# Moving the second half of each tile's projection later in a mixer's attention, and leaving out twelve products of constants

## The chip, the cores and the metric

The kernel runs on one core of one Trainium2 chip. The metric is the device time of one execution in microseconds (us).

## The reference

The model has two layers (DEPTH = 2) on 512 rows of width 1024. Each layer is a half-step feed-forward net, a mixer, and a second half-step feed-forward net, all with RMS norms around them:

```python
h = h + 0.5 * rms_norm(swiglu(rms_norm(h, g[0]), ffn1_gate[l], ffn1_up[l], ffn1_down[l]), g[1])
m = hybrid_mixer(rms_norm(h, g[2]), w_in[l], ...)
h = h + rms_norm(m, g[3])
h = h + 0.5 * rms_norm(swiglu(rms_norm(h, g[4]), ffn2_gate[l], ffn2_up[l], ffn2_down[l]), g[5])

def hybrid_mixer(u, w_in, ...):
    proj = u @ w_in                                   # 1024 -> 1796 columns
    qa, ka, va, us, qc, kc, vc, fc = jnp.split(proj, IN_SPLITS, axis=-1)
    ya = swa_sink_attention(qa, ka, va, ...)          # 8 heads, sliding window of 2 chunks of 64
    yb = s5_mixer(us, ...)                            # state-space layer, GELU and a gate (GLU)
    yc = fox_attention(qc, kc, vc, fc, ...)           # 4 heads, causal, with forget gates
    y = jnp.concatenate([rms_norm(ya, ga), rms_norm(yb, gb), rms_norm(yc, gc)], axis=-1)
    return y @ w_out
```

## The kernel before, in words

Everything is written by hand for each engine, in program order, with counting semaphores between the engines. Activations lie transposed in SBUF. Each weight is split into a high part (`wh`, ScalarE, L1046) and a low part (`wl`, VectorE, L1494), and each product of weights and activations is done as three (`three`: L559, L560, L561) into one PSUM bank, so a tile of 128 output columns is 8 steps of k with three products of 512 columns each. Most of the time goes to such products in the feed-forward nets.

The mixer's input projection has 15 column tiles (`COLS`). Tiles 0 to 8 are projected ahead of the attention. Tiles 9 to 14 (`vc0`, `kc0`, `qc0`, `kc1`, `vc1`, `qc1`: what the forgetting attention needs) are projected inside the attention loop, each as two halves of k, 12 products each (`project_half`). All six use the same PSUM bank, `ps1`, one after the other: the first half of a tile waits in `bank_free` for the semaphore that VectorE raises (L1692) when its reader of the tile before is done. The reader is `value_columns` (L1720, for `vc0` and `vc1`) or `fox_tile` (L1732, two operations, for the others).

The loop over `s` runs through 32 items of attention, 16 of the sliding window (`swa`: four head pairs by four blocks of 128 queries) and 16 of the forgetting attention (`fox`), and some steps beyond. TensorE does at step s: the scores of item s (L847 and L851, or L855 and L857, or L863 and L865), halves of tiles by table, `attend` (L905, at odd s for two items that started four and five steps earlier), and the transpose of the probabilities of item s − 3 (`turn`, L882). VectorE does the maximum of item s (L1782 to L1791 and L1795) and the normalisation of item s − 2 (L1805 to L1814), then readers, splits and parts of the state-space layer. ScalarE does the copy of the transposed probabilities of item s − 3 (L1277), the exponentials of item s (L1257 and L1262, or L1266), then copies, splits and more. The scores of item s wait for the exponentials of item s − 2, since two banks alternate. Between the items stand the state-space layer's products: `ssm_direct` at step 2 (L812, L815), `ssm_out` at step 4 (L825), whose copy by ScalarE (L1350) the scores of item 6 wait for, the gate (`glu`, L942) at step 17, and a norm's sum (`branch_sum`, L930) at step 22. At step 3 twelve products of constants into a bank that nobody reads (`spin`, L605) stand before the transpose.

Tables set what stands at which step: `PROJECT_AT` the first halves (items 0, 4, 8, 12, 16, 19). The second half of a tile stands one step after the first, its reader and the ScalarE split of a later tile's weights two steps after the first, on VectorE and ScalarE:

```python
if s in PROJECT_AT:
    project_half(PROJECT_AT[s], 0)
if s - 1 in PROJECT_AT:
    project_half(PROJECT_AT[s - 1], 1)
...
if half == 0:
    bank_free(m)
    pe.wait_ge(w_split, base + u + RAW_SLOTS + 1)
```

Of the kernel before, what the change touches and what calls it, by code (L numbers as in the profile page):

```python
# [75 lines left out]
N_COLS = len(COLS)  # L76
# [11 lines left out]
def units_of(m):  # L88

    return (m, 1) if m < TILE["fc"] else (m, 2) if m == TILE["fc"] else (m + 1, 1)  # L90
# [94 lines left out]
def build(nc, x, norm_gains, ffn1_gate, ffn1_up, ffn1_down, w_in, swa_sinks, lam_re, lam_im, log_dt,  # L185
# [8 lines left out]
    with ExitStack() as ctx:  # L194
# [332 lines left out]
        def _(pe):  # L527
# [227 lines left out]
            def mixer(l):  # L755
# [15 lines left out]
                def project_half(m, half):  # L771

                    b, place = bank_of(m)
                    u = units_of(m)[0]
# [3 lines that stand above are left out]
                    for k in range(half * (KD // 2), (half + 1) * (KD // 2)):  # L778
                        mm = three(ps[b][:, :], in_slot(u), k, k, k == 0, k == KD - 1)
                    if half:  # L780
                        mm.then_inc(unit_done, 1)
# [193 lines left out]
                for s in range(N_ITEMS + LAG_PV):  # L975
                    if s == SSM_OUT_AT - 2:
                        ssm_direct()
                    if s == SSM_OUT_AT:
                        ssm_out()
                    if s < N_ITEMS:  # L980
                        scores(s)
                    if s in PROJECT_AT:
                        project_half(PROJECT_AT[s], 0)
                    if s - 1 in PROJECT_AT:
                        project_half(PROJECT_AT[s - 1], 1)
                    if s in SPIN_AT:
                        spin(BU_BANK[0], SPIN_AT[s])
                    if s > LAG_PV and (s - LAG_PV) % 2:
                        attend(s - LAG_PV - 1)
                    if LAG_T <= s < N_ITEMS + LAG_T:  # L990
                        turn(s - LAG_T)
                    if s in VALUES_AT:
                        values(VALUES_AT.index(s))
                    if s in SUM_AT:
                        branch_sum(SUM_AT[s])
                    if s in OUT_AT:
                        out_part(0, OUT_AT[s])
                    if s == 29:
                        fox_sum(6)
                    if s == GLU_AT:  # L1000
                        glu()
# [19 lines left out]
        def _(act):  # L1021
# [185 lines left out]
            def mixer(l):  # L1207
# [29 lines left out]
                for u in range(5, N_AHEAD + 3):  # L1237
                    if u > 6:
                        split_unit(base + u, in_slot(u))
                    m = u - 3  # L1240
# [92 lines left out]
                for s in range(N_ITEMS + LAG_PV):  # L1333
# [6 lines left out]
                            pair_out(pr)  # L1340
                    if s in VALUES_AT:
                        values(VALUES_AT.index(s))
                    if s - 2 in PROJECT_AT and PROJECT_AT[s - 2] + 2 < N_COLS:
                        u = units_of(PROJECT_AT[s - 2] + 2)[0]
                        split_unit(base + u, in_slot(u))
                    if s == SSM_OUT_AT:
                        act.wait_ge(o_mm, l + 1)
# [69 lines left out]
        def _(dve):  # L1417
# [260 lines left out]
            def mixer(l):  # L1678
# [165 lines left out]
                for u in range(5, N_AHEAD + 3):  # L1844
# [3 lines left out]
                    m = u - 3  # L1848
# [22 lines left out]
                for s_ in range(N_ITEMS + LAG_N):  # L1871
                    if s_ < N_ITEMS:
                        maxes(s_)
                    if s_ >= LAG_N:
                        norms(s_ - LAG_N)
                    if s_ - 2 in PROJECT_AT:
                        m = PROJECT_AT[s_ - 2]
                        if COLS[m][0][0] == "v":
                            value_columns(m, 1 + int(COLS[m][0][2]))
                        else:  # L1880
                            fox_tile(m, [n_ for n_, _ in COLS if n_[:2] in ("kc", "qc")].index(COLS[m][0]))
# [314 lines left out]
SPLIT_BEHIND = {0: (4, 5), 4: (6,), 5: (7,)}  # L2196
OUT_SPLIT_AT = {21: 0, 22: 1, 30: 2, 31: 3}
OUT_AT = {27: (0,), 28: (1,), 29: (2,), 30: (3,), 31: (4,), 32: (5,)}
SPIN_HOLE, SPIN_AT = 18, {3: 12}
PAD = 24  # L2200
ROWS_FROM = 6

# [3 lines left out]
GELU_AT = (7, 11)  # L2206
GLU_AT = 17
GATE_STEPS = {1: ((0, 0),), 2: ((0, 1), (1, 0)), 3: ((0, 2), (1, 1)), 4: ((1, 2),)}
LOW_AT = {3: 11, 8: 12, 12: 13, 15: 14}
PROJECT_AT = {0: 9, 4: 10, 8: 11, 12: 12, 16: 13, 19: 14}  # L2210
VALUES_AT = (None, 8, 20)

# [26 lines left out]
```

## Time and profile before

| | |
|---|---|
| time, median of 3 runs (lowest, highest) | 1948.27 us (1942.56, 1949.94) |
| the profiled execution: its time, its span | 1947.21 us, 1945.3 us |
| TensorE busy | 98% of the span |
| VectorE, ScalarE, GpSimd busy | 52%, 37%, 11% |
| mean granted clock of TensorE | 0.990 of full speed |
| TensorE's share of the chain that ended last | 95% |

The span is the time from the first to the last instruction; the device time is some 2 us longer. The chain that ended last is followed back from the last instruction through whatever released each step. A granted clock of 1.0 is TensorE's upper level (2.4 GHz), 0.5 its lower (1.2 GHz).

### The profile page before, as it was taken

The page shows a single profiled execution, that of the slowest core. Times are in us where ns is not written, and L with a number is a line of the kernel's source. Part 1 is how long each engine was busy: PE and PEld are TensorE (multiplying, and loading weights), DVE is VectorE, ACT ScalarE, POOL GpSimd, SP SyncE. Part 2 cuts the span into 40 slices and gives each one's busy share as a digit, 9 for nine tenths or more (in the row PEclk, how much of TensorE's full clock was granted, in tenths as well). Part 3 has the DMA queues.
Part 4 walks back from the last instruction along what each step waited for, and adds up shares of the span by engine and source line. Part 5 has one row for each costly group of instructions (what it writes and reads, how often), then busy time and mean ns, then how long its engine had stood idle before and what let it go on. Part 6 is the DMA issues. An engine that isn't in the chain of part 4 may idle for free.

```text
span 1945.3 us, 24754 instructions
## 1 busy us (share of the span) xinstructions
PE 1909.2 (98%) x9136; PEld 1543.7 (79%) x9136; DVE 1006.3 (52%) x1429; ACT 723.1 (37%) x1134; POOL 209.9 (11%) x433
## 2 busy tenths in 40 slices
PE   8999999999999999999999999999998999999998
PEld 6888888877667888888878888887875778888887
DVE  5664432387657544432376544335876574444323
ACT  4333332255654433332243333223565453333321
POOL 2831000023100000000056100000131000000000
PEclk9999999999999999999999999999998999999999
DMA  6334343351213333343333433333502123333331
GB/s 176 108 106 127 97 119 98 85 158 55 55 46 85 104 95 96 96 118 102 99 89 98 131 98 109 105 94 98 161 25 66 55 86 99 97 97 104 109 90 44
DMA packets 330954, 188.55 MB, mean 97 GB/s; under 512 B 6996, under 2 KB 325432, under 8 KB 329848
## 3 DMA queue, kind: packets, MB, share of 16 engines
q1 hardware_dynamic: 324008, 168.13, 30.1%
q0 software_dynamic: 5824, 18.79, 3.5%
q8 instruction: 52, 0.85, 0.2%
q10 hardware_dynamic: 1040, 0.52, 0.1%
q14 instruction: 30, 0.25, 0.0%
HBM read 175.72 MB, written 11.67 MB: 96 GB/s over the span
## 4 chain that ended last, share of the span: by engine, by line
PE 95%; ACT 2%; DVE 2%; issue 1%; DMA 0%; DVEq 0%; ACTq 0%
PE ps L559 19%; PE ps L561 18%; PE ps L560 18%; PE ps L696 8%; PE ps L695 8%; PE ps L694 8%; PE ps L587 2%; PE ps L588 2%; PE ps L592 2%; PE ps L905 1%; PE ps L882 1%; PE ps L863 1%; DMA raw<-in_ffn_gate 0%; PE ps L639 0%; PE ps L855 0%
## 5 line engine op out<-in xcount | busy, mean ns | idle before, releaser
L1494 DVE TENSOR_TENSOR wl<-raw,wh 128x1024 fp32r<-128x1024 f32 (+1 forms) x265 | 350.6, 1324 | 755.9 <-ACT wh L1046 754.7
L559 PE MATMUL ps<-xh,wh 128*128 128x512 f32 x1552 | 612.4, 395 | 2.4 <-DVEq L1692 1.3
L561 PE MATMUL ps<-xh,wl 128*128 128x512 f32 x1552 | 605.3, 390 | 0.0
L560 PE MATMUL ps<-xl,wh 128*128 128x512 f32 x1552 | 605.2, 390 | 0.0
L1046 ACT ACTIVATE wh<-raw 128x1024 fp32r<-128x1024 f32 (+1 forms) x265 | 301.1, 1137 | 658.7 <-PE ps L696 341.6
L559 PEld LDWEIGHTS ps<-xh,wh 128*128 128x128 f32 x1552 | 292.0, 188 | 67.9 <-issue 3.5
L561 PEld LDWEIGHTS ps<-xh,wl 128*128 128x128 f32 x1552 | 291.8, 188 | 61.6
L560 PEld LDWEIGHTS ps<-xl,wh 128*128 128x128 f32 x1552 | 292.1, 188 | 60.1 <-issue 1.2
L694 PE MATMUL ps<-Hh,wh 128*128 128x512 f32 x704 | 274.0, 389 | 0.0
L696 PE MATMUL ps<-Hh,wl 128*128 128x512 f32 x704 | 273.9, 389 | 0.0
L695 PE MATMUL ps<-Hl,wh 128*128 128x512 f32 x704 | 273.9, 389 | 0.0
L695 PEld LDWEIGHTS ps<-Hl,wh 128*128 128x128 f32 x704 | 132.1, 188 | 27.6
L696 PEld LDWEIGHTS ps<-Hh,wl 128*128 128x128 f32 x704 | 132.1, 188 | 27.3
L694 PEld LDWEIGHTS ps<-Hh,wh 128*128 128x128 f32 x704 | 132.1, 188 | 27.3
L1141 ACT ACTIVATE Hh<-full 128x512 fp32r<-128x512 f32 (+1 forms) x88 | 55.6, 632 | 167.2 <-DVE full L1568 167.2
L1137 ACT ACTIVATE sig<-sig 128x512 f32<-128x512 f32 x88 | 55.6, 632 | 147.3 <-DVE sig L1558 147.3
L1558 DVE TENSOR_TENSOR sig<-ps,rstd 128x512 f32<-128x512 f32 x88 | 60.2, 684 | 12.4 <-ACT rstd L1060 11.2
L1561 DVE TENSOR_TENSOR sig<-sig,rstd 128x512 f32<-128x512 f32 x88 | 62.2, 707 | 7.1
L1575 DVE TENSOR_TENSOR Hl<-full,Hh 128x512 fp32r<-128x512 f32 (+1 forms) x88 | 60.2, 685 | 2.8 <-ACT Hh L1141 2.8
L1568 DVE TENSOR_TENSOR full<-ps,sig 128x512 f32<-128x512 f32 x88 | 60.1, 683 | 1.8 <-PE ps L561 1.4
L1277 ACT ACTIVATE probT<-ps 128x256 f32<-128x256 f32 (+3 forms) x64 | 31.4, 491 | 67.8 <-PE ps L882 67.8
L2063 POOL MEMSET dskT<- 32x16 f32 x2 | 0.2, 106 | 493.6 <-PE ps L696 460.0
(327 smaller groups left out, 1803.7 us busy)
## 6 DMA issues: line engine op xcount, KB each, us to landing
raw<-in_ffn_up SPq DMA_DIRECT2D x88, 512.0 KB, 3.8
raw<-in_ffn_down SPq DMA_DIRECT2D x64, 704.0 KB, 4.6
raw<-in_ffn_gate SPq DMA_DIRECT2D x87, 512.0 KB, 3.8
raw<-in_w_in SPq DMA_DIRECT2D x28, 512.0 KB, 4.8
raw<-in_w_out SPq DMA_DIRECT2D x16, 512.0 KB, 3.9
xrow<-in_x SPq DMA_DIRECT2D x2, 1024.0 KB, 8.7
ssm_t<-evict POOLq DMA_DIRECT2D x8, 256.0 KB, 3.1
ssm_v<-evict POOLq DMA_DIRECT2D x8, 256.0 KB, 2.7
```

Source lines behind the costliest of these rows:

```text
L559: pe.matmul(bank, w_tile(True, slot, kw), xh[:, kx, :], start=first, stop=False)
L560: pe.matmul(bank, w_tile(True, slot, kw), xl[:, kx, :], start=False, stop=False)
L561: return pe.matmul(bank, w_tile(False, slot, kw), xh[:, kx, :], start=False, stop=last)
L694: pe.matmul(bank, wh[:, slot, k, :], Hh[:, f, :], start=(f == 0), stop=False)
L695: pe.matmul(bank, wh[:, slot, k, :], Hl[:, f, :], start=False, stop=False)
L696: mm = pe.matmul(bank, wl[:, slot, k, :], Hh[:, f, :], start=False, stop=(f == KF - 1))
L1046: act.activation(w_high(slot, k0, nk), raw[:, slot4, 0:nk - k0, :], ACT.Copy).then_inc(w_hi, 1)
L1494: V.tensor_tensor(w_low(slot, k0, nk), raw[:, slot4, 0:nk - k0, :], w_high(slot, k0, nk).bitcast(F32), ALU.subtract).then_inc(w_split, 1)
L1558: V.tensor_tensor(sig[:, 0, :], ps[2 * b][:, :], rstd[:, :], ALU.mult).then_inc(si_v, 1)
L1561: V.tensor_tensor(sig[:, 1, :], sig[:, 1, :], rstd[:, :], ALU.mult).then_inc(si_v, 1)
L1568: V.tensor_tensor(full[:, fb, :], ps[2 * b + 1][:, :], sig[:, 1, :], ALU.mult).then_inc(h_full, 1)
L1575: V.tensor_tensor(Hl[:, f_slice, :], full[:, b:b + 1, :], Hh[:, f_slice, :].bitcast(F32), ALU.subtract).then_inc(h_lo, 1)
```

## The change

Two tables of their own set the steps of the second halves (`SECOND_AT`) and of what follows them (`DONE_AT`: the reader on VectorE and the split on ScalarE). The second half of tiles 9 to 12 stands two steps after the first instead of one (items 2, 6, 10, 14), their readers three steps after instead of two (items 3, 7, 11, 15). Tile 13 keeps its places (half at 17, reader at 18). Tile 14's second half goes from item 20 to 21, its reader from 21 to 22. The low part of the weights of tiles 11 and 14 (`LOW_AT`) goes from items 3 and 15 to 4 and 16, behind the ScalarE split. The twelve products of constants at item 3 are gone. First halves stay where they were. No instruction is added.

```diff
--- before.py
+++ after.py
@@ -981,8 +981,8 @@
                         scores(s)
                     if s in PROJECT_AT:
                         project_half(PROJECT_AT[s], 0)
-                    if s - 1 in PROJECT_AT:
-                        project_half(PROJECT_AT[s - 1], 1)
+                    if s in SECOND_AT:
+                        project_half(SECOND_AT[s], 1)
                     if s in SPIN_AT:
                         spin(BU_BANK[0], SPIN_AT[s])
                     if s > LAG_PV and (s - LAG_PV) % 2:
@@ -1340,8 +1340,8 @@
                             pair_out(pr)
                     if s in VALUES_AT:
                         values(VALUES_AT.index(s))
-                    if s - 2 in PROJECT_AT and PROJECT_AT[s - 2] + 2 < N_COLS:
-                        u = units_of(PROJECT_AT[s - 2] + 2)[0]
+                    if s in DONE_AT and DONE_AT[s] + 2 < N_COLS:
+                        u = units_of(DONE_AT[s] + 2)[0]
                         split_unit(base + u, in_slot(u))
                     if s == SSM_OUT_AT:
                         act.wait_ge(o_mm, l + 1)
@@ -1873,8 +1873,8 @@
                         maxes(s_)
                     if s_ >= LAG_N:
                         norms(s_ - LAG_N)
-                    if s_ - 2 in PROJECT_AT:
-                        m = PROJECT_AT[s_ - 2]
+                    if s_ in DONE_AT:
+                        m = DONE_AT[s_]
                         if COLS[m][0][0] == "v":
                             value_columns(m, 1 + int(COLS[m][0][2]))
                         else:
@@ -2196,7 +2196,9 @@
 SPLIT_BEHIND = {0: (4, 5), 4: (6,), 5: (7,)}
 OUT_SPLIT_AT = {21: 0, 22: 1, 30: 2, 31: 3}
 OUT_AT = {27: (0,), 28: (1,), 29: (2,), 30: (3,), 31: (4,), 32: (5,)}
-SPIN_HOLE, SPIN_AT = 18, {3: 12}
+SPIN_HOLE, SPIN_AT = 18, {}
+SECOND_AT = {2: 9, 6: 10, 10: 11, 14: 12, 17: 13, 21: 14}
+DONE_AT = {3: 9, 7: 10, 11: 11, 15: 12, 18: 13, 22: 14}
 PAD = 24
 ROWS_FROM = 6
 
@@ -2206,7 +2208,7 @@
 GELU_AT = (7, 11)
 GLU_AT = 17
 GATE_STEPS = {1: ((0, 0),), 2: ((0, 1), (1, 0)), 3: ((0, 2), (1, 1)), 4: ((1, 2),)}
-LOW_AT = {3: 11, 8: 12, 12: 13, 15: 14}
+LOW_AT = {4: 11, 8: 12, 12: 13, 16: 14}
 PROJECT_AT = {0: 9, 4: 10, 8: 11, 12: 12, 16: 13, 19: 14}
 VALUES_AT = (None, 8, 20)
```

On TensorE, in the first layer at items 1 and 2: the half of tile 9 (L559 to L561, here without its repetitions) stood ahead of the direct product of the state-space layer (L812, L815).

```order
 L855 MATMUL ps<-kz,qa 128x256
 L857 MATMUL ps<-maskb,identb 128x256
-L559 MATMUL ps<-xh,wh 128x512
-L560 MATMUL ps<-xl,wh 128x512
-L561 MATMUL ps<-xh,wl 128x512
...
 L812 MATMUL ps<-maskb 128x512 x2
 L815 MATMUL ps<-u,tmat 128x64 x16
```

It now stands behind the scores of item 2 (L855, L857), and the constants (L605) are gone from before the transpose of item 0 (L882):

```order
+L559 MATMUL ps<-xh,wh 128x512
+L560 MATMUL ps<-xl,wh 128x512
+L561 MATMUL ps<-xh,wl 128x512
...
 L855 MATMUL ps<-kz,qa 128x256
 L857 MATMUL ps<-maskb,identb 128x256
-L605 MATMUL ps<-maskb,identb 128x384 x12
 L882 MATMUL ps<-ident,prob 128x128 x2
 L825 MATMUL ps<-hst,cmat 128x63 x32
```

On VectorE, in the first layer at items 6 and 7: the reader of tile 10 (L1732, `kf`) stood behind the softmax of item 6, and now stands behind the maximum (L1782 to L1784) of item 7 and the normalisation (L1805 to L1810) of item 5.

```order
 L1807 TENSOR_SCALAR prob<-prob,stat 128x128
 L1810 TENSOR_SCALAR prob<-prob,stat 128x128
+L1782 TENSOR_REDUCE stat<-ps 128x1
+L1783 TENSOR_REDUCE stat<-ps 128x1
+L1784 TENSOR_TENSOR stat<-stat,nsinks 128x2
+L1805 TENSOR_TENSOR stat<-stat 128x2
+L1806 RECIPROCAL stat<-stat 128x2
+L1807 TENSOR_SCALAR prob<-prob,stat 128x256
+L1810 TENSOR_SCALAR prob<-prob,stat 128x256
 L1732 SCALAR_TENSOR_TENSOR kf<-ps,rstd 64x512 x2
```

What follows on VectorE there (L1890, part of the GELU) is as before; the reader of tile 11 moves in the same way at items 10 and 11, that of tile 12 at items 14 and 15.

On VectorE, in the first layer at items 21 and 22: the reader of tile 14 (L1732, `qf`) stood before the gate's first product (L1912), and now stands behind the softmax of item 22.

```order
-L1732 SCALAR_TENSOR_TENSOR qf<-ps,rstd 64x512 x2
 L1912 TENSOR_TENSOR yB<-us,gst 128x8x64
 L1925 TENSOR_TENSOR acc<-acc,sq 128x512
...
 L1813 RECIPROCAL stat<-stat 128x1
 L1814 TENSOR_SCALAR prob<-prob,stat 128x384
+L1732 SCALAR_TENSOR_TENSOR qf<-ps,rstd 64x512 x2
 L1912 TENSOR_TENSOR yB<-us,gst 128x8x64
```

It moved past the gate's first product, the norm's sum (L1925) and one softmax. SyncE's queue is the same in both.

## Rows read from the trace of the kernel before

**Rows 1.** The page: busy time (share) and instructions by engine; chain by engine

```profile
PE 1909.2 (98%) x9136; PEld 1543.7 (79%) x9136; DVE 1006.3 (52%) x1429; ACT 723.1 (37%) x1134; POOL 209.9 (11%) x433
...
PE 95%; ACT 2%; DVE 2%; issue 1%; DMA 0%; DVEq 0%; ACTq 0%
```

**Rows 2.** TensorE's waits, 445 to 562 us: us in total, times, longest

```profile
PE ps L905 <- ACT probT L1277: 2.0, 3, 1.6
PE ps L847 <- ACT stat L1262: 1.7, 3, 0.6
PE ps L930 <- DVE acc L1925: 1.5, 1, 1.5
PE ps L882 <- DVE prob L1814: 1.0, 1, 1.0
PE ps L882 <- ACT probT L1277: 0.6, 1, 0.6
PE ps L559 <- DVEq L1692: 0.6, 1, 0.6
```

**Rows 3.** Stretches: length, TensorE busy (instructions), granted clock, DMA share, GB/s

```profile
530.20:541.20 11.00, 6.26 (x41) 0.88 0.26 77
539.76:545.50 5.74, 5.74 (x25) 0.51 0.31 91
1491.60:1504.70 13.10, 11.67 (x43) 0.51 0.28 80
```

**Rows 4.** Timeline, items 1 to 4, first layer: start, us, engine, line, operation [idle]

```profile
449.38 0.48 PE L559 MATMUL ps<-xh,wh 128*128 128x512 f32 x1
...
452.30 0.60 PE L812 MATMUL ps<-maskb 32*128 32x512 bf16 x2
...
456.45 0.65 PE L855 MATMUL ps<-kz,qa 128*128 128x256 f32 x2
...
458.87 2.11 PE L605 MATMUL ps<-maskb,identb 128*128 128x384 bf16 x12
461.46 0.44 PE L882 MATMUL ps<-ident,prob 128*128 128x128 f32 x2 [0.47 <-DVE prob L1810]
...
466.23 0.48 PE L559 MATMUL ps<-xh,wh 128*128 128x512 f32 x1
...
455.72 0.47 ACT L1262 ACTIVATE stat<-sinks,stat 128x1 f32<-128x1 f32 x2
...
460.09 1.31 DVE L1810 TENSOR_SCALAR prob<-prob,stat 128x128 f32<-128x128 f32 x1
```

**Rows 5.** Timeline, items 6 to 8 of the first layer, TensorE, ScalarE and VectorE

```profile
474.83 0.70 PE L847 MATMUL ps<-kz,qa 64*128 64x256 f32 x4
...
475.68 0.63 PE L882 MATMUL ps<-ident,prob 128*128 128x128 f32 x4
...
476.86 0.70 PE L847 MATMUL ps<-kz,qa 64*128 64x256 f32 x4 [0.56 <-ACT stat L1262]
...
479.47 0.50 PE L559 MATMUL ps<-xh,wh 128*128 128x512 f32 x1
...
471.26 1.09 ACT L1350 ACTIVATE u<-ps 128x512 f32<-128x512 f32 x2
...
475.68 0.42 DVE L1782 TENSOR_REDUCE stat<-ps 128x1 f32<-128x256 f32 x1 [3.02 <-PE ps L851]
...
477.33 1.40 DVE L1732 SCALAR_TENSOR_TENSOR kf<-ps,rstd 64x512 f32<-64x512 f32 x2
478.89 0.42 DVE L1782 TENSOR_REDUCE stat<-ps 128x1 f32<-128x256 f32 x1 [0.15 <-DVE kf L1732]
...
480.68 0.68 DVE L1890 TENSOR_TENSOR sig<-u 128x512 f32<-128x512 f32 x1
```

**Rows 6.** Timeline of VectorE, items 21 to 23 of the first layer

```profile
529.71 1.40 DVE L1732 SCALAR_TENSOR_TENSOR qf<-ps,rstd 64x512 f32<-64x512 f32 x2
...
536.87 0.42 DVE L1814 TENSOR_SCALAR prob<-prob,stat 128x384 f32<-128x384 f32 x1
```

## The prediction, made before the changed kernel ran

> **What bounds the kernel now.** I read the page first. TensorE is busy for 98% of the span and is 95% of the chain that ended last [rows 1], so time comes only from work taken off TensorE, from holes in it, or from its clock. Nothing on its own instruction list is changed except one group of fillers. So I read the mixer's attention on TensorE in order of time, where the change lies, in the first layer (up to item 22 the second layer's rows repeat it). The list of TensorE's waits there shows 7.4 us of holes in 117 us in its six largest rows [rows 2], and each belongs to a place: L847 before the scores of items 7, 11 and 15 (three times 0.56, ScalarE's exponentials late), L559 before the first half of the last tile at item 19 (0.6, the projection bank not free), L930 at item 22 (1.5, VectorE's sum), L882 at items 22 and 24 (0.6, 1.0) and L905 at item 25 (1.6). The other quantity is the clock: it is at its upper level up to item 24, then falls; from 539.76 to 545.5 the granted clock is 0.51 in the first layer, and in the second it is 0.51 for 13.1 us from 1491.6 [rows 3]. In both layers TensorE had been idle between thin instructions just before.
>
> **The change, part by part.** Distances are taken from start to start in the timeline, which holds the small issue gaps too.
>
> *The constants' products.* The 12 products per layer (L605) stand at 458.87 and are followed by the transpose of item 0 at 461.46, which waited for VectorE's probabilities, written from 460.09 for 1.31, so to 461.40 [rows 4]. Removing them can't bring that transpose forward. Value: nothing in itself.
>
> *The half of tile 9, items 1 to 2.* It took 449.38 to 452.30, 2.9 us. Without it there the direct product of the state-space part (L812, L815) starts at about 449.4 and ends at about 453.5. Then the scores of item 2 need the exponentials of item 0, whose last row on ScalarE starts at 455.72 and takes 0.47: 456.2, against 456.45 before. So 2.7 us of the 2.9 become a hole. The half then runs behind the scores of item 2, in the place of the constants (2.1 us) and of the wait behind them (0.5), and the transpose of item 0 stands at 461.4 as before. Net 0. The cover that is gone is activity: dense products used to stand where now nothing does for 2.7 us.
>
> *Its reader and the split of tile 11.* The reader (L1720, VectorE) goes from before to after the softmax of item 1 and ends at about 464.1; tile 10's half, which needs the bank, starts at 466.23 [rows 4], so it is hidden by the state-space output product. The split goes one item later on ScalarE and VectorE, which both wait there for TensorE; tile 11 is projected at item 8, 8 us later. Nothing. SP's queue issues the same loads in the same order.
>
> *The half of tile 10, items 5 to 6.* TensorE leaves item 5 about 2.9 us earlier and comes to the scores of item 6 at 471.9; but these wait for ScalarE's copies of the state-space output (471.26 + 1.09 = 472.35) [rows 5]. 0.45 is lost again, and the 0.7 between the transpose of item 3 and the scores of item 7 closes (475.68 + 0.5 to 476.86) because the half now gives ScalarE time. Net −0.25. The same at items 9 to 11 and 13 to 15 without the wait for the copies: −0.7 each.
>
> *The readers of tiles 10, 11 and 12: the term that decides.* All tiles from 9 on share one bank, and the first half of the next tile at items 8, 12 and 16 waits until the reader is done. Before, the reader ran in VectorE's item 6 (477.33) and the half started at 479.47 with 0.6 us to spare [rows 5]. Now it stands behind the softmax of item 7, and that can't start before the scores of item 7. From these: 0.85 until VectorE starts (474.83 to 475.68, item 6's rows), 1.79 for maximum and normalisation (478.89 to 480.68), 1.56 for the reader (477.33 to 478.89), 4.2 in all. TensorE needs 476.86 to 479.47, 2.6, from the same scores to the half. A wait of 1.6 us arises. Items 12 and 16 repeat these rows: 3 × 1.6 = 4.8 us per layer.
>
> *Tile 13* keeps its places, and its 0.6 wait at item 19.
>
> *The half of tile 14, items 20 to 21.* The scores of item 21 come 2.9 us earlier against their surroundings and feed ScalarE and VectorE. The holes behind (L882's 0.6 and L930's 1.5 at item 22 [rows 2]; 2.4 with the issue gaps beside them, as 0.7 above stands for a wait of 0.56) close: −2.4. But the reader (1.56, at 529.71 before) moves to item 22 on VectorE, which from there to the probabilities of item 21 (536.87 + 0.42, which L882 awaits) has no idle time [rows 6]; what it did while the gate was computed on ScalarE it now does later. +1.5 at item 24. From item 24 on nothing is shifted.
>
> Sum per layer: 4.8 − 0.25 − 1.4 − 2.4 + 1.5 = +2.25; two layers **+4.5 us**.
>
> *The clock.* The trace has no hole as long as the new 2.7 us, so I bound it. Lower bound: it holds, 0. Upper: as at item 24 of the first layer, where idle times of 1.0 and then 1.6 us with thin instructions between them were enough, and the rows after were at half rate for 5.7 us [rows 3]; at half rate 5.7 us hold 2.9 us of lost work. Behind the new hole stand 5 us of dense work (scores, the half, scores) with nothing to hide the loss. I take 2.5 per fall. On the other hand 530 to 541 had 4.7 us of idle time in 11 before the clock gave way, so a single hole need not do it. I give even chances per layer and put one fall in the forecast: **+2.5 us**. The page "TensorE: Matmul & The Clock Gate" of the Trainium skill, section "Why this matters for your kernels", warns of idle gaps between bursts that are longer than the one worked out here. By it the clock would stay up at this place and the sum would end at +4.5. The rows at item 24 speak against leaning on that, since no single gap there was as long as this one.
>
> The profiled execution took 1947.2 us (span 1945.3) and the median of the runs shown is 1948.3, 1.1 above. With the terms on the median: 1948.3 + 4.5 + 2.5 = 1955.3, so **1955 us**.
>
> **The rivals.**
> 1. *The bank waits come, the clock holds.* For it: in items 1 to 22 no hole so far cost the clock. 1948.3 + 4.5 = 1952.8. This is the case by the skill's rule above.
> 2. *The clock falls more often*: in both layers at item 2, and at some of the six bank waits, each of which is 1.6 us idle behind thin transposes and attention products, much like the place where it fell before. A fall there slows the half behind it, 2.8 us of work, so costs up to 2.8; I take 1.7. Two falls at item 2 and two to four at waits: 4.5 + 5 + 3.4 to 6.8 gives 1961 to 1965. Against it: 0.56 us holes at items 7, 11, 15 left it alone.
> 3. *The other side, faster: the reader is in time.* If VectorE reaches the reader of tiles 10 to 12 within the 2.6 us that TensorE needs, instead of 4.2, the three waits are not there and only what closes remains: 2.25 − 4.8 = −2.55 per layer, 1943. It decides at 1.6 us saved in VectorE's chain. For it speaks only that VectorE waited 3.0 us for the scores of item 6 before; but the chain starts at the scores of item 7, not at VectorE's backlog, and that is against it.
> 4. *It comes to nothing*: the late holes (1.0 and 1.6 at items 24 and 25) swallow the delay, as they would if VectorE and ScalarE and not TensorE paced items 20 to 25 already. Then about −2.2 per layer against +2.25: 1948. Against it: with the shift of 3 us at item 20 the whole pipeline behind comes later with it.
>
> **How the numbers follow.** Forecast case (waits and about one fall) 0.38; rival 1 0.22; rival 2 0.27; rival 3 0.06; rival 4 0.07. The range 1947 to 1963 leaves out rival 3 and the upper end of rival 2; the likeliest case by itself is 1952 to 1958. A measurement of this kernel can tell about 0.5%, 9.7 us: slower than 1958 takes rival 2 and the top of the forecast's own range, 0.32; faster than 1938.5 would need more than rival 3 gives, 0.04; the rest, 0.64, is no change.
>
> **What would show it.** In the profile after: TensorE idle for about 2.7 us before the scores of item 2 (releaser ScalarE), the transpose of item 0 at 461.4; three new waits of L559 for VectorE's bank release (L1692), 1.5 to 1.9 us each, so six and the two old ones over both layers; the waits of L847 before items 7, 11, 15 gone; L930's wait gone and L882's at item 24 near 2.7; item 24's scores some 2 us later relative to item 0. Granted clock: a stretch near 0.5 after 456 in one layer. I am wrong if L559's waits stay at 0.6 (then the reader chain was mis-sized), or if the clock rows differ from one fall.

## The result, and the profile after

| | median | lowest to highest | runs |
|---|---|---|---|
| kernel before, beside it | 1945.73 us | 1936.95 to 1950.83 | 20 |
| changed kernel | 1950.70 us | 1948.26 to 1953.66 | 20 |

The ratio is 1.0028, its 95% interval 1.0016 to 1.0039. The changed kernel is 5.0 us slower: a small difference that is clear of noise, within the 0.5% that I called no change, and inside the forecast's range of 1947 to 1963, though below the 1952 to 1958 that I called likeliest. The profiled execution took 1952.14 us (span 1950.3 us, mean granted clock 0.989).

The page of the changed kernel, busy time by engine and the chain that ended last by engine, answers to [rows 1]:

```profile
PE 1905.0 (98%) x9112; PEld 1544.5 (79%) x9112; DVE 1008.1 (52%) x1429; ACT 721.7 (37%) x1134; POOL 209.7 (11%) x433
...
PE 90%; DVE 6%; ACT 3%; issue 1%; DMA 0%; DVEq 0%; ACTq 0%
```

TensorE has 24 products fewer (the constants) and is still 98% busy. VectorE went from 2% to 6% of the chain: TensorE now waits for it at places where it did not before. Which places, the list of TensorE's waits in the first layer's attention (445 to 566 us) says; it answers to [rows 2]:

```profile
PE ps L559 <- DVEq L1692: 5.2, 4, 1.6
PE ps L882 <- DVE prob L1814: 2.8, 1, 2.8
PE ps L855 <- ACT stat L1262: 2.3, 1, 2.3
PE ps L905 <- ACT probT L1277: 1.2, 2, 1.0
```

The first row is the bank of the projection: once 0.6 us before, four times and 5.2 us in all now. The third row is the hole before the scores of item 2. The three waits of L847 for ScalarE and the one of L930 for VectorE are gone. The timeline of TensorE at these places:

```profile
448.88 0.38 PE L855 MATMUL ps<-kz,qa 128*128 128x128 f32 x2
...
454.00 3.79 PE L815 MATMUL ps<-u,tmat 128*128 128x64 f32 x32
460.04 0.70 PE L855 MATMUL ps<-kz,qa 128*128 128x256 f32 x2 [2.25 <-ACT stat L1262]
...
461.57 0.63 PE L560 MATMUL ps<-xl,wh 128*128 128x512 f32 x1
...
464.88 0.40 PE L559 MATMUL ps<-xh,wh 128*128 128x512 f32 x1
...
466.65 0.38 PE L882 MATMUL ps<-ident,prob 128*128 128x128 f32 x2
...
481.72 0.70 PE L847 MATMUL ps<-kz,qa 64*128 64x256 f32 x4
...
485.87 0.50 PE L559 MATMUL ps<-xh,wh 128*128 128x512 f32 x1 [1.46 <-DVEq L1692]
...
514.07 0.50 PE L559 MATMUL ps<-xh,wh 128*128 128x512 f32 x1 [1.64 <-DVEq L1692]
...
538.30 1.02 PE L930 MATMUL ps<-acc,ones 128*128 128x512 f32 x2
...
544.41 0.90 PE L882 MATMUL ps<-ident,prob 128*128 128x128 f32 x3 [2.82 <-DVE prob L1814]
...
1419.28 0.70 PE L855 MATMUL ps<-kz,qa 128*128 128x256 f32 x2 [2.64 <-ACT stat L1262]
...
1426.22 3.79 PE L825 MATMUL ps<-hst,cmat 64*128 64x63 f32 x64
```

The last two rows are of the second layer: its hole before the scores of item 2, and its state-space output products. Most products of the half behind the hole take 0.63 us each, where they take 0.40 from 464.88 on: the clock is at its lower level there. VectorE's timeline at item 7 is the other side of the bank wait at 485.87; its rows before are in [rows 5]:

```profile
482.57 0.42 DVE L1782 TENSOR_REDUCE stat<-ps 128x1 f32<-128x256 f32 x1 [2.39 <-PE ps L851]
...
484.36 1.40 DVE L1732 SCALAR_TENSOR_TENSOR kf<-ps,rstd 64x512 f32<-64x512 f32 x2
485.91 0.69 DVE L1890 TENSOR_TENSOR sig<-u 128x512 f32<-128x512 f32 x1 [0.15 <-DVE kf L1732]
```

From the scores of item 7 (481.72) it is 0.85 to the maximum, 1.79 to the reader and 1.55 to its end, 4.2 us; the half starts at 485.87, as the bank comes free. VectorE itself was idle for 2.39 us in front of that chain: it was not short of time, its reader was queued behind work that had no input yet.

Stretches of TensorE (length, busy, granted clock, DMA share, GB/s) around the hole, in either layer, and the part of the first in which the clock is down:

```profile
456.00:466.00 10.00, 7.75 (x38) 0.83 0.01 3
1410.00:1426.00 16.00, 13.36 (x71) 0.89 0.13 34
...
461.33:464.75 3.42, 3.42 (x10) 0.50 0.00 0
```

The clock fell behind the hole in both layers; in the first it was at 0.50 for 3.4 us, from 1.3 us after the hole's end. The kernel before, at the three places that the table below needs, in its first layer:

```profile
444.97 0.27 PE L855 MATMUL ps<-kz,qa 128*128 128x128 f32 x1
...
532.92 1.12 PE L930 MATMUL ps<-acc,ones 128*128 128x512 f32 x2 [1.49 <-DVE acc L1925]
...
537.34 0.55 PE L882 MATMUL ps<-ident,prob 128*128 128x128 f32 x3 [1.03 <-DVE prob L1814]
```

The start of the first scores moves by several us between executions (443.5 to 448.9), with nothing changed ahead of them, so all comparisons below are distances from them. They are differences of starts in the timeline: to the transpose of item 0 (L882; 466.65 − 448.88 = 17.77), to the norm's sum at item 22 (L930), to the second sum at item 25, and to the end of the mixer (the first L605 behind it). Layer one / layer two, us:

| kernel | transpose, item 0 | sum, item 22 | sum, item 25 | end of mixer |
|---|---|---|---|---|
| before | 16.5 / 16.8 | 88.0 / 88.3 | 97.2 / 99.8 | 160.5 / 162.2 |
| before, again | 16.4 / 16.8 | 88.0 / 88.2 | 96.1 / 96.3 | 157.9 / 158.1 |
| after | 17.8 / 18.2 | 89.4 / 89.8 | 100.3 / 100.8 | 162.5 / 162.8 |
| after, again | 17.8 / 18.2 | 91.1 / 91.7 | 102.1 / 102.7 | 164.7 / 164.8 |
| e1, no constants | 16.4 / 16.7 | 91.1 / 93.1 | 102.6 / 104.7 | 165.1 / 167.5 |
| e2, tile 9 | 17.8 / 18.2 | 90.0 / 90.1 | 101.5 / 101.6 | 164.2 / 164.4 |
| e3, tiles 10 to 12 | 16.5 / 16.8 | 90.6 / 90.9 | 102.1 / 102.5 | 165.0 / 164.9 |
| e4, readers in old places | 17.8 / 18.2 | 84.6 / 86.4 | 95.5 / 97.3 | 158.2 / 160.5 |
| e4, again | 17.9 / 17.9 | 84.8 / 86.4 | 95.7 / 97.3 | 157.9 / 160.3 |
| e5, tile 14 | 16.4 / 16.8 | 85.8 / 86.3 | 96.7 / 97.2 | 160.2 / 159.3 |
| e6, hole filled | 16.5 / 16.9 | 88.1 / 90.2 | 99.0 / 101.1 | 161.4 / 164.0 |
| e7, best of the parts | 16.4 / 16.8 | 83.5 / 84.1 | 94.4 / 95.0 | 157.2 / 157.7 |
| e7, again | 16.4 / 16.7 | 83.3 / 84.2 | 94.2 / 95.1 | 157.6 / 158.2 |
| e8, and late constants | 16.4 / 16.8 | 83.3 / 84.0 | 93.1 / 93.8 | 154.9 / 155.5 |

The first column shows the clock's loss at item 2, the second minus the first the items 3 to 22 (bank waits, closed gaps, and falls of the clock there), the third minus the second the late holes.

### The profile page after: what moved, and what is told of

It reads as the page before. It is cut to its first block, busy times and chain, and to the rows that moved or that the text cites. A ratio compares the mean times of both kernels' runs of the same rounds, so it can differ in the third digit from the quotient of the medians.

```text
span 1950.3 us, 24706 instructions
## 1 busy us (share of the span) xinstructions
PE 1905.0 (98%) x9112; PEld 1544.5 (79%) x9112; DVE 1008.1 (52%) x1429; ACT 721.7 (37%) x1134; POOL 209.7 (11%) x433
## 4 chain that ended last, share of the span: by engine, by line
PE 90%; DVE 6%; ACT 3%; issue 1%; DMA 0%; DVEq 0%; ACTq 0%
PE ps L559 18%; PE ps L560 17%; PE ps L561 17%; PE ps L696 8%; PE ps L694 8%; PE ps L695 8%; PE ps L587 2%; PE ps L588 2%; PE ps L592 2%; PE ps L882 1%; PE ps L905 1%; PE ps L863 1%; DVE wl L1494 1%; ACT sig L1218 0%; DMA raw<-in_ffn_gate 0%
## 5 line engine op out<-in xcount | busy, mean ns | idle before, releaser
L559 PE MATMUL ps<-xh,wh 128*128 128x512 f32 x1552 | 614.4, 396 | 11.5 <-DVEq L1692 10.4
L561 PE MATMUL ps<-xh,wl 128*128 128x512 f32 x1552 | 607.1, 391 | 0.0
L559 PEld LDWEIGHTS ps<-xh,wh 128*128 128x128 f32 x1552 | 293.3, 189 | 78.7 <-DVEq L1692 12.4
L561 PEld LDWEIGHTS ps<-xh,wl 128*128 128x128 f32 x1552 | 293.0, 189 | 62.2
```

The source lines that it names most:

```text
L559: pe.matmul(bank, w_tile(True, slot, kw), xh[:, kx, :], start=first, stop=False)
L561: return pe.matmul(bank, w_tile(False, slot, kw), xh[:, kx, :], start=False, stop=last)
```

## The experiments

There were two theories. The first was that the reader's place makes the bank wait and that this is most of the loss; the rival was that the clock, brought down by the hole at item 2, is the larger part. In the edits below a table not shown is as in the changed kernel. The kernel before ran beside each group: e1 to e4 at 1944.96 us, e5 to e7 and its repeat at 1944.88, e8 and the repeat of after at 1942.55, and the repeats of e4 and e7 at 1945.07.

**e1: the kernel before, only without the products of constants.**

```diff
-SPIN_HOLE, SPIN_AT = 18, {3: 12}
+SPIN_HOLE, SPIN_AT = 18, {}
```

> The kernel before without the twelve products of constants at item 3; nothing else is changed. The wait theory: they end 0.5 us before the transpose of item 0 can run, so time and places stay, 0 us. The clock theory: they keep TensorE active there; with a 2.6 us hole before that transpose in their place the granted clock falls in the stretch from 457 to 466 as it did in the changed kernel (0.81 there), and the state-space output product behind it, whose rows are short, loses up to 1 us per layer, 0 to 2 us in all.

Measured 1954.34 us (1950.90 to 1957.01, 6 runs) against 1944.96, ratio 1.0052 (1.0038 to 1.0066). This is 9.4 us slower, more than the whole change costs, and neither theory had said so. The timeline around item 3 of this kernel:

```profile
461.60 0.44 PE L882 MATMUL ps<-ident,prob 128*128 128x128 f32 x2 [2.41 <-DVE prob L1810]
461.97 5.28 PE L825 MATMUL ps<-hst,cmat 64*128 64x63 f32 x64
```

The transpose is where it was, as I had worked out (16.4 in the table). But TensorE is idle for 2.41 us before it, and what follows runs at the lower clock: the state-space output products take 5.28 us, and the second layer of the changed kernel has 3.79 for the same 64. The stretches:

```profile
462.00:472.00 10.00, 10.00 (x82) 0.66 0.19 55
1422.00:1434.00 12.00, 12.00 (x84) 0.57 0.16 45
```

By item 22 the delay is 3.1 and 4.9 us, 8.0 for both layers. The other 1.4 of the 9.4 lie behind item 22, where executions differ (below). The products of constants write nothing that is read and bring nothing forward; they kept the clock up.

**e2: only tile 9's half moved (and no constants, as in the change).**

```diff
-SECOND_AT = {2: 9, 6: 10, 10: 11, 14: 12, 17: 13, 21: 14}
-DONE_AT = {3: 9, 7: 10, 11: 11, 15: 12, 18: 13, 22: 14}
+SECOND_AT = {2: 9, 5: 10, 9: 11, 13: 12, 17: 13, 20: 14}
+DONE_AT = {3: 9, 6: 10, 10: 11, 14: 12, 18: 13, 21: 14}
...
-LOW_AT = {4: 11, 8: 12, 12: 13, 16: 14}
+LOW_AT = {4: 11, 8: 12, 12: 13, 15: 14}
```

> Tile 9's half, reader and split moved one item later and no constants, as in the changed kernel; tiles 10 to 14 as before. If the hole before the scores of item 2 costs the clock and only that, the transpose of item 0 comes 1.3 to 1.4 us late in each layer as in the changed kernel, everything behind it too: +2.7 us. If the bank waits were all of the changed kernel's loss, 0 us.

Measured 1950.36 us (1947.48 to 1953.00, 6 runs), ratio 1.0031 (1.0019 to 1.0044): 5.4 us. The clock behind the hole is down in both layers:

```profile
456.00:462.00 6.00, 5.54 (x18) 0.72 0.00 0
1416.00:1422.00 6.00, 6.00 (x22) 0.73 0.00 0
```

At the transpose this costs 1.3 and 1.4 us, 2.7 in all, what was expected; by item 22 it is 2.0 and 1.8, of which 0.5 in the first layer is a wait of the gate's products for a DMA. The median is another 1.6 above these 3.8. So it is a little over half of e1's loss: the moved half fills the wait in which the constants stood, and opens a hole of 2.26 us elsewhere, behind which less is lost.

**e3: only tiles 10 to 12 moved, with the constants kept.**

```diff
-SPIN_HOLE, SPIN_AT = 18, {}
-SECOND_AT = {2: 9, 6: 10, 10: 11, 14: 12, 17: 13, 21: 14}
-DONE_AT = {3: 9, 7: 10, 11: 11, 15: 12, 18: 13, 22: 14}
+SPIN_HOLE, SPIN_AT = 18, {3: 12}
+SECOND_AT = {1: 9, 6: 10, 10: 11, 14: 12, 17: 13, 20: 14}
+DONE_AT = {2: 9, 7: 10, 11: 11, 15: 12, 18: 13, 21: 14}
...
-LOW_AT = {4: 11, 8: 12, 12: 13, 16: 14}
+LOW_AT = {3: 11, 8: 12, 12: 13, 16: 14}
```

> Halves of tiles 10 to 12 moved one item later with their readers and splits as in the changed kernel; tile 9, tile 14 and the constants as before. The bank theory: three waits of 1.45 to 1.65 us per layer against 0.9 to 1.9 us of closed holes: +2.7 to 3.1 us per layer up to item 20, with nothing given back by tile 14, so +5.5 to 6 us, more than the whole change. The rival, that VectorE's and ScalarE's later waits absorb the bank waits, gives +1 us or less.

Measured 1951.45 us (1950.21 to 1954.72, 5 runs), ratio 1.0041 (1.0027 to 1.0054): 6.5 us. Its list of TensorE's waits, 445 to 562 us, repeats the row of the changed kernel to the tenth:

```profile
PE ps L559 <- DVEq L1692: 5.2, 4, 1.6
```

By item 22 the delay is 2.7 and 2.6 us: three new waits, 4.5 us per layer together, less some 1.9 of closed holes. The clock stayed up at these waits in both layers.

**e4: the changed kernel with VectorE's readers of tiles 10 to 12 back at the items where they stood.** The halves stay where the change put them.

```diff
-                    if s_ in DONE_AT:
-                        m = DONE_AT[s_]
+                    if s_ in READ_AT:
+                        m = READ_AT[s_]
...
+READ_AT = {3: 9, 6: 10, 10: 11, 14: 12, 18: 13, 22: 14}
```

> The changed kernel with VectorE's readers of tiles 10 to 12 back at items 6, 10 and 14, where they now wait for the half that TensorE does in the same item; halves and splits stay in the new places. The bank theory: the reader ends before TensorE reaches the next tile, the waits of L559 at items 8, 12 and 16 are gone, and the holes that closed stay closed: 4.9 us per layer less than the changed kernel, so about 1941 where that has 1950.7, and faster than before by about 3 us even with the clock's loss at item 2. The rival, that the reader now stalls VectorE (it waits about 2 us for the half at items 6, 10, 14) and the maximum of the next item comes late, gives the time of the changed kernel within 2 us.

Measured 1939.98 us (1937.99 to 1943.45, 11 runs), ratio to before 0.9977 (0.9967 to 0.9987): 10.7 us below the changed kernel's median, 9.9 by the two ratios to the kernel before. Its repeat, e4 again below, gave 1939.12 (1937.43 to 1945.02, 7 runs), ratio 0.9973 (0.9958 to 0.9988). TensorE's waits for the bank are back to the one at item 19, and now VectorE waits. TensorE's waits and VectorE's timeline at item 6:

```profile
PE ps L559 <- DVEq L1692: 0.6, 1, 0.6
```

```profile
480.68 1.41 DVE L1732 SCALAR_TENSOR_TENSOR kf<-ps,rstd 64x512 f32<-64x512 f32 x2 [1.23 <-PE ps L561]
```

The reader waits 1.23 us for the half that now ends later, on an engine that has the time, and the bank is free before TensorE asks for it. The reader's place on VectorE alone turns the change from slower into faster. The expected and the measured time differ by 1 us. TensorE's waits in the second layer (1401 to 1488 us) show what is late next:

```profile
PE ps L855 <- ACT stat L1262: 2.7, 1, 2.7
PE ps L942 <- DMA us<-mix_y: 1.2, 1, 1.2
```

The gate's products (L942) now come before their data, which a DMA brings; TensorE does not wait for it in the kernel before. In the repeat it is 1.5 us. This is 1.2 of the 1.8 us by which this kernel's second layer stands behind its first at the sum of item 22 (86.4 against 84.6).

**e5: only tile 14 moved, with the constants kept.**

```diff
-SPIN_HOLE, SPIN_AT = 18, {}
-SECOND_AT = {2: 9, 6: 10, 10: 11, 14: 12, 17: 13, 21: 14}
-DONE_AT = {3: 9, 7: 10, 11: 11, 15: 12, 18: 13, 22: 14}
+SPIN_HOLE, SPIN_AT = 18, {3: 12}
+SECOND_AT = {1: 9, 5: 10, 9: 11, 13: 12, 17: 13, 21: 14}
+DONE_AT = {2: 9, 6: 10, 10: 11, 14: 12, 18: 13, 22: 14}
...
-LOW_AT = {4: 11, 8: 12, 12: 13, 16: 14}
+LOW_AT = {3: 11, 8: 12, 12: 13, 15: 14}
```

> Tile 14's half at item 21 and its reader at item 22, all else as before. The wait theory: the waits of item 22 (0.6 and 1.5 us) close and about two thirds come back as a wait at item 24, since VectorE does the reader later: 1 us per layer less, and the late loss of the clock, where before its norm's sum ran at the lower level, gets shorter by 1 us per layer as in the changed kernel: 2 to 4 us faster in all. The rival, that the place of tile 14 makes no difference and the changed kernel gave back nothing there: 0 us.

Measured 1942.84 us (1941.22 to 1946.30, 12 runs) against 1944.88, ratio 0.9991 (0.9979 to 1.0002): 2.0 us less, and the interval includes no difference. The profile is plainer than the median: the sum of item 22 comes 2.1 and 2.0 us earlier than in the kernel before, and the transpose of item 24 gives most of it back:

```profile
535.72 0.55 PE L882 MATMUL ps<-ident,prob 128*128 128x128 f32 x3 [2.82 <-DVE prob L1814]
```

Its wait is 2.82 us, against 1.03 at the same place before. The transpose stands 91.92 us behind the first scores, and stood at 92.37, so 0.45 of the 2.1 us is left there.

**e6: the changed kernel with twelve products of constants in the hole at item 2.**

```diff
                     if s == SSM_OUT_AT - 2:
                         ssm_direct()
+                        spin(BU_BANK[0], 12)
                     if s == SSM_OUT_AT:
```

> The changed kernel with twelve products of constants per layer in the new hole, ahead of the scores of item 2. The clock theory: they take 2.1 of the 2.3 to 2.6 us of the hole, the granted clock stays at 1.00 from 456 to 466, and the transpose of item 0 comes 16.5 us after the first scores instead of 17.8 and 18.2: 2.6 to 2.8 us less than the changed kernel, about 1948. The rival, that the late transpose comes from the order of the instructions and not from the clock: 1950.7, no change.

Measured 1946.46 us (1942.86 to 1949.57, 12 runs), ratio to before 1.0011 (0.9999 to 1.0022), 4.2 us under the changed kernel's median. By the ratios it is 3.3, and the two intervals overlap. The clock stays up at both places, and the transposes are back at 16.5 and 16.9. The same two stretches as above, and one of the second layer around a bank wait of 1.66 us at 1465.96:

```profile
456.00:466.00 10.00, 9.58 (x93) 1.00 0.01 2
1410.00:1426.00 16.00, 15.15 (x125) 1.00 0.00 1
...
1460.00:1480.00 20.00, 18.34 (x101) 0.91 0.38 89
```

What was won at item 2 of the second layer was lost again at that wait (90.2 at the sum of item 22, against 88.1 in the first layer), so the filler mends one place, and the clock can still fall at another.

**e7: what was good of each part**: constants kept, tile 9 as before, halves of tiles 10 to 12 and 14 moved, readers of 10 to 12 in their old places (by e4's edit, whose first part is not shown again).

```diff
-SPIN_HOLE, SPIN_AT = 18, {}
-SECOND_AT = {2: 9, 6: 10, 10: 11, 14: 12, 17: 13, 21: 14}
-DONE_AT = {3: 9, 7: 10, 11: 11, 15: 12, 18: 13, 22: 14}
+SPIN_HOLE, SPIN_AT = 18, {3: 12}
+SECOND_AT = {1: 9, 6: 10, 10: 11, 14: 12, 17: 13, 21: 14}
+DONE_AT = {2: 9, 7: 10, 11: 11, 15: 12, 18: 13, 22: 14}
+READ_AT = {2: 9, 6: 10, 10: 11, 14: 12, 18: 13, 22: 14}
...
-LOW_AT = {4: 11, 8: 12, 12: 13, 16: 14}
+LOW_AT = {3: 11, 8: 12, 12: 13, 16: 14}
```

> Tile 9 and the constants as before; halves and splits of tiles 10 to 12 one item later but their VectorE readers at the old items 6, 10 and 14; tile 14 as in the changed kernel. No hole at item 2, no bank waits, holes at items 7, 11, 15 and 22 closed: 2.9 us per layer less than before and 2.6 us less than the version with tile 9 moved and no constants (1940.0), so 1937 to 1939. If the clock's loss at item 2 was not worth anything by itself: 1940.

Measured 1939.61 us (1935.71 to 1944.02, 12 runs), ratio 0.9977 (0.9965 to 0.9990). It is level with e4, where I had expected some 2.6 us less (1937 to 1939).

**The kernel before, again**, to see how much one kernel's profile differs from itself.

> The kernel before once more, for a second profile of it: no change. Time from the first scores to the end of the mixer 160 to 162.5 us in each layer, and the late fall of the clock from item 24 on as in the first profile or, if it varies between executions, 1 to 2 us longer in the first layer, where the first profile has less of it than the second layer.

Measured 1945.05 us (1936.85 to 1950.64, 12 runs), ratio 1.0004 (0.9992 to 1.0016). Its profiled execution has a span of 1935.0 us, where the first had 1945.3. Up to item 22 the two agree to 0.1 us. Behind it they don't. Stretches of the first profile:

```profile
534.00:550.00 16.00, 13.18 (x80) 0.79 0.23 67
1490.00:1506.00 16.00, 13.14 (x54) 0.57 0.23 66
```

and of the second:

```profile
534.00:550.00 16.00, 13.16 (x95) 1.00 0.23 67
1490.00:1506.00 16.00, 14.19 (x90) 1.00 0.23 66
```

In the first layer the waits are the same in both (0.63 and 1.49 at item 22, 1.03 and 1.59 at items 24 and 25), and once the clock gives way and once it doesn't. In the second layer of the first profile it gave way earlier, in the wait before the sum of item 22, which then took 2.07 us:

```profile
1491.65 2.07 PE L930 MATMUL ps<-acc,ones 128*128 128x512 f32 x2 [1.49 <-DVE acc L1925]
```

The second profile has that wait of 1.49 too, and the one of 0.63 in front of it, at a clock of 1.00. The mixers are 6.7 us shorter without the falls (315.9 against 322.7 for both). Another 3.2 us of the difference of the spans lie between the mixers, where the clock fell at 1112 in the first profile and not in the second; more on that place under e7 again.

**e8: e7 with 14 and 5 products of constants in the holes at items 24 and 25.**

```diff
-                        spin(BU_BANK[0], SPIN_AT[s])
+                        spin(BU_BANK[s > 3], SPIN_AT[s])
...
-SPIN_HOLE, SPIN_AT = 18, {3: 12}
+SPIN_HOLE, SPIN_AT = 18, {3: 12, 24: 14, 25: 5}
```

> The version with VectorE's readers at the old items, tile 9 and the constants as before (1939.6), plus fourteen products of constants per layer in the wait of item 24 ahead of the transpose (2.8 us long there) and five at item 25 ahead of the attention's product. The clock theory: the late fall of the granted clock, which slows TensorE from about 535 to 542 there, does not come; the second norm's sum takes 1.0 us instead of 1.9, and some 2 us per layer are saved: 1935 to 1937. The rival, that the constants are as much in the way as they help, or that the clock's fall there is hidden by the waits for VectorE and ScalarE: 1939 to 1941.

Measured 1934.34 us (1932.51 to 1936.92, 6 runs) against 1942.55, ratio 0.9954 (0.9937 to 0.9972). This is faster than the kernel before and than the changed one, which ran beside it at 1950.80 (below). The kernel before beside it was 2.3 to 2.5 us faster than beside e7, so the gain over e7 is better read from the ratios: 0.9977 and 0.9982 for e7, 4.5 to 5.4 us, with intervals that overlap at their ends. In the profiles the mixers are 4.4 and 5.4 us shorter than in e7's two (310.4 against 314.9 and 315.8), the same size. Its times lie within 4.4 us (6 runs), those of the kernel before beside it within 10.5 (1937.31 to 1947.76, 16 runs). TensorE's timeline there, first layer:

```profile
533.20 2.44 PE L605 MATMUL ps<-maskb,identb 128*128 128x384 bf16 x14
536.19 0.55 PE L882 MATMUL ps<-ident,prob 128*128 128x128 f32 x3 [0.55 <-DVE prob L1814]
...
538.61 0.88 PE L905 MATMUL ps<-probT,vc 128*64 128x128 f32 x12 [0.78 <-ACT probT L1277]
```

The attention products take 0.88 us for twelve, where e5 beside its 2.82 us hole has 1.55. The stretches around the two places:

```profile
520.00:540.00 20.00, 18.67 (x123) 1.00 0.14 42
1480.00:1500.00 20.00, 18.47 (x122) 1.00 0.19 53
```

The clock fell late in the mixer in 24 of the 26 layers of all other profiles, and here in neither. The two others without a fall are those of the kernel before, again, so two layers of one profile support the theory and do not prove it.

**The changed kernel, again.**

> The changed kernel once more, for a second profile: 1950 to 1951. The waits of L559, three of 1.45 to 1.65 us per layer and the old one of 0.63, and the hole at item 2 are in the program and stay to within 0.1 us; the fall of the clock at item 2 (a chance of the hole in the first profile, or its rule) comes again in both layers if it is the rule; the start of the first scores, 448.9, moves to 444 to 446 if the 3.9 us ahead of the mixer were chance.

Measured 1950.80 us (1948.16 to 1953.19, 11 runs) against 1942.55, ratio 1.0037 (1.0026 to 1.0049). The profile has the same waits and the same fall at item 2, and one fall more in each layer, at places of the bank waits:

```profile
500.00:520.00 20.00, 18.35 (x105) 0.91 0.44 106
1440.00:1460.00 20.00, 18.21 (x114) 0.91 0.09 27
```

In the first layer it is behind the wait of 1.65 us at item 16, in the second behind the one of 1.45 at item 12. They cost 1.7 and 1.9 us at the sum of item 22 (table).

**e7 again**, on one chip with e4 again, since the two had come out level.

> The version with readers at the old items and tile 9 and the constants as before, once more, beside the one with tile 9 moved and no constants on the same chip: if the clock's fall at item 2 costs what the late transposes show, it is 2.6 us below that one. If the 0.3 us between their medians on two occasions was right, they are the same, and the late falls of the clock make up for it.

> The version with readers at the old items, tile 9 moved and no constants, once more: 1940, and the first transposes 17.8 and 18.2 us after the first scores, since the hole at item 2 has brought the clock down in all profiles so far.

Measured: e7 1941.88 us (1936.51 to 1943.86, 11 runs), ratio 0.9982 (0.9971 to 0.9994); e4 1939.12 as above. In the profiles e7 has its transposes 1.5 and 1.2 us earlier and its mixers 2.4 us shorter (315.8 against 318.2 for both), and its median is 2.8 us longer. So is its profiled span: 1940.1 against 1937.3. The difference lies outside the mixers, where the two programs are the same. Before the first mixer e7 takes 2.0 us more, and between the mixers 3.15. There 64 products of 64x16 stand (L639). The row is e7's; e4 has 3.75 us for the same 64. The stretch around them, first in e7 and then in e4, has no idle time in either:

```profile
1108.14 4.50 PE L639 MATMUL ps<-cT,bbd 64*128 64x16 f32 x64
...
1104.00:1124.00 20.00, 20.00 (x123) 0.83 0.52 123
...
1104.00:1124.00 20.00, 20.00 (x136) 1.00 0.52 116
```

The time between the mixers is 794.7 to 794.8 us in the nine profiles without a fall at this place and 797.9 in four of the five with one (796.3 in the fifth, the changed kernel's first). The same products stand at 153 to 154 us, and there too the granted clock falls in e7 (0.77 from 150 to 165) and not in e4. So what e7 wins at item 2 is there in its profile, and the clock takes more than that back at places that the edits don't touch.

## Why the prediction was right, and where it wasn't

**The bank waits, the term that decides: right.** Predicted was a chain of 4.2 us from the scores against 2.6 for TensorE, 1.6 us three times per layer. Measured are 4.2 and waits of 1.46, 1.46 and 1.64 beside the old 0.63 (5.2 for four). e3 makes them (+6.5 us, with the closed holes against them) and e4 takes them away alone (−10.7). Of e4's gain 4.8 and 3.4 us, 8.3 in all, are to be seen by item 22 against the changed kernel's first profile; the three new waits are 4.6 per layer, 9.1, and the gate's wait for its data takes 1.2 back. Against its second profile, in which the clock fell at a bank wait in each layer, it is 11.9. Where the rest of the 10.7 lies is not shown; such falls may be part of it.

**Items 5 to 15, −1.65 per layer, and the late holes, −2.4 and +1.5: right in kind, the late pair somewhat too good.** L847's and L930's waits are gone, and L882 waits 2.82 at item 24, forecast near 2.7. e3 has the −1.65 as some −1.9. e5 has the −2.4 as −2.1 and −2.0, and the +1.5 as +1.7, so 0.45 is won in the first layer where 0.9 was forecast. The whole up to item 24: its transpose stands at 544.41 − 448.88 = 95.53, and stood at 537.34 − 444.97 = 92.37, so +3.16. Of this 1.28 is the clock at item 2 (17.77 − 16.49), and 1.88 is left for the terms that I had summed to 2.25. This also refuses rival 4, that the late holes swallow the delay: at the sum of item 25 it is still 3.15.

**Rival 3, the reader in time: refused by the trace, and made true by e4.** It asked for a reader that is done 1.6 us earlier. e4 is 5.0 us below the kernel before, where this rival had 5.1; but e4 pays for the clock at item 2 besides, which the rival did not count.

**The clock at item 2: right in sum, wrong in how it comes.** I had a hole of 2.7 us and even chances per layer at 2.5 a fall, so +2.5. The hole is 2.25 and 2.64 us, up to 2.72 in the other profiles. The clock fell in every layer of every profile that has the hole (after twice, e2, e4 twice: 10 of 10), and in none where the place was filled (before twice, e3, e5, e6, e7 twice, e8: 16). A fall costs 1.3 and 1.4 at the transpose in the changed kernel (1.2 to 1.5 over all ten), 2.7 for both layers. The chance was too low, the price too high, and that they cancelled is luck. The step that failed in the price is the bound: the rows at item 24 were at half rate for 5.7 us, and here the granted clock was 0.50 for 3.4 us (461.33 to 464.75), so at most 1.7 us of work could be lost. The step that failed in the chance is the reading of the trace before. I went by item 24 because no hole was as long as 2.7 us, but at the kernel's start there is one close to it, with the clock at its lower level right behind it:

```profile
12.25 0.47 PE L587 MATMUL ps<-xh,wh 128*128 128x512 f32 x1 [2.45 <-DVE wl L1494]
...
12.90:19.70 6.80, 5.86 (x16) 0.50 0.91 244
```

And that "in items 1 to 22 no hole so far cost the clock" held for the first layer alone: in the second the fall came in the wait of 1.49 at item 22 (1491.65), and not at item 24. The page "TensorE: Matmul & The Clock Gate" of the Trainium skill, section "Why this matters for your kernels", warns of longer gaps than these; by it rival 1, 1952.8, would have been the mechanism. The trace disagrees with it in all ten layers (holes of 2.25 to 2.72 us).

**The constants: "value: nothing in itself" failed, by its cover.** The transpose did not come forward, as worked out. But the products were priced as work in a wait, and not as what keeps the clock: e1 without them loses 9.4 us, 8.0 of it to be seen by item 22. In the changed kernel this price is not paid, because the half of tile 9 comes to stand in the same wait. That this made the step's sum right is luck too; as the value of those 24 products "nothing" is 9 us out.

**Rival 2, falls at bank waits: true in part.** The first profile of the changed kernel has none, the second one per layer, at 1.7 and 1.9 us, which is the 1.7 that I took. e6 shows one, e3 none: 3 of the 8 layers with these waits, too few to say how often they come.

**The point itself**: the sum was 1955.3, measured is 1950.7. The base explains 2.5 of the 4.6 us (1948.3 from three runs, 1945.7 from twenty). The forecast of the difference was 7.0; measured were 5.0, and 8.3 in the last comparison. Up to item 24 the profiles show 6.5 for both layers (3.2 and, against the second profile of before, 3.3), so the near hit of the median is not luck alone.

**What stays open.** Falls of the clock differ between executions of one kernel, late in the mixers and also outside them, so one profile carries up to 10 us that another doesn't (the two of the kernel before: 6.7 in the mixers, 3.2 between them). Why the clock gives way in one execution and not in the next no run shows. e2's median is 1.6 above what its profile shows by item 22, and e6's gain over the changed kernel is 4.2 where 2.7 was its place's price; falls at other places may be the reason, which is not shown. What the fall at item 2 is worth in the median once the bank waits are gone was not settled: the medians of e7 and e4 are equal in one comparison (12 and 11 runs), and in the other (11 and 7 runs) e7 is 2.8 us longer.

## What to carry to other kernels

When a producer's half is moved later, ask for each reader that moves with it what it is now queued behind: a reader behind a softmax whose scores haven't been issued waits for them, and its bank with it, however idle the engine is. Price filler products by what the clock does without them, not by the time they fill; take them out alone before counting them as free. And where a clock fall comes and goes between executions, profile the same kernel twice before explaining a difference of that size, and compare the parts that the edit did not touch before saying that profile and median disagree.

## What the runs showed that I had not expected

- One idle time of 2.25 to 2.72 us, behind thin products, came with a fall of the clock from 2.4 to 1.2 GHz in 10 of 10 layers, and one of 2.41 us without the constants in both layers of e1. At bank waits of 1.45 to 1.66 us it fell at one place per layer in one of the changed kernel's two profiles, at one in e6 and at none in e3.
- With the same program, the stretch behind items 22 to 24 ran once at 0.79 and 0.57 of the granted clock and once at 1.00: 6.7 us of mixer, about half of the 1937 to 1951 us over which the kernel before spreads.
- The clock also fell with no idle time at all, at 64 products of 64x16 (L639) between the mixers, in 5 of 14 profiles, at 3.2 us in four of them.
- Twelve small bf16 products, 2.1 us of TensorE's time per layer that compute nothing, are worth 9.4 us at item 3; 19 more at items 24 and 25 (2.44 and 0.97 us) took the ratio to the kernel before from e7's 0.9977 or 0.9982 to 0.9954, and the spread of the times from 8.3 us (12 runs) to 4.4 (6 runs, and fewer runs spread less).
- The first scores of the first layer start anywhere from 443.5 to 448.9 us, with the same instructions ahead of them in all these kernels; a fall of the clock at 155 to 158 us, behind the same 64x16 products, is there in 8 of the 14 profiles.
